# The opening of a 256-token block: constant matmuls while waiting, an early table load, and another order of the first units and pieces

## The reference, cut to what matters here

```python
def rms_norm(x, g):
    return x * rsqrt(mean(x * x) + 1e-6) * g

h = rms_norm(x, a_norm)                    # x: (1, 256, 1024)
u, z = split(h @ a_w_in, 2)                # a_w_in: 1024 x 2048
# pooled = windowed means of u, minus u
x = x + (mixed(pooled) * silu(z)) @ a_w_out
...                                        # gates, attention, S5, two MLPs follow
```

## Time and profile before

| | us |
|---|---|
| median of 3 runs | 898.32 |
| lowest and highest run | 893.40 and 901.04 |
| span of the profiled execution | 892.2 |

### The profile page before, as it was taken

One profiled execution on the slowest core, in us unless ns is written; L12 is line 12 of the kernel. 1 busy time (PEld: TensorE's weight loads), 2 busy tenths in 40 slices (PEclk: granted clock), 3 DMA queues, 4 the chain that ended last, 5 costly groups with the idle time before them and its releaser, 6 DMA issues.

```text
span 892.2 us, 13365 instructions
## 1 busy us (share of the span) xinstructions
PE 855.0 (96%) x5611; PEld 739.6 (83%) x5611; DVE 589.4 (66%) x739; ACT 441.0 (49%) x585; POOL 106.8 (12%) x73
## 2 busy tenths in 40 slices
PE   6999999899999999999899999997889999999998
PEld 4886888788788877878888888996778889999996
DVE  4684575676756668877768788774875655555553
ACT  5644466655953646644544445452064544444441
POOL 1000000211000013123033334330000000000000
PEclk9999999999999999999999999999899999999999
DMA  8936645365104436226455566557866555555521
GB/s 294 358 103 230 240 142 189 110 230 183 45 10 161 155 95 243 87 96 212 142 187 163 206 225 210 181 203 163 263 211 208 170 189 190 188 189 189 189 95 48
DMA packets 67253, 155.96 MB, mean 175 GB/s; under 512 B 3017, under 2 KB 6826, under 8 KB 66938
## 3 DMA queue, kind: packets, MB, share of 16 engines
q1 hardware_dynamic: 63888, 146.28, 48.7%
q0 software_dynamic: 2224, 7.67, 2.6%
q10 hardware_dynamic: 1082, 1.16, 0.6%
HBM read 146.70 MB, written 7.34 MB: 173 GB/s over the span
## 4 chain that ended last, share of the span: by engine, by line
PE 84%; DVE 10%; ACT 3%; DMA 2%; issue 1%; POOL 1%; ACTq 0%; DVEq 0%
PE bank L677 17%; PE bank L678 17%; PE bank L679 17%; PE bank L987 7%; PE bank L989 7%; PE bank L991 7%; PE bank L670 2%; PE bank L772 2%; DVE wlo L1572 2%; DVE wlo L1567 1%; DVE hT L1555 1%; ACT whi L1209 1%; PE bank L1052 1%; PE bank L762 1%; POOL rsh L2214 1%
## 5 line engine op out<-in xcount | busy, mean ns | idle before, releaser
L1572 DVE TENSOR_TENSOR wlo<-ring,whi 128x2048 fp32r<-128x2048 f32 (+1 forms) x105 | 256.9, 2450 | 141.7 <-ACT whi L1209 141.4
L1209 ACT ACTIVATE whi<-ring 128x2048 fp32r<-128x2048 f32 (+1 forms) x105 | 200.5, 1909 | 215.6 <-PE bank L679 147.8
L677 PE MATMUL bank<-whi,hT 128*128 128x512 f32 (+1 forms) x512 | 202.2, 395 | 5.1 <-DVE hT L2180 2.3
L679 PE MATMUL bank<-whi,hT 128*128 128x512 f32 (+1 forms) x512 | 199.8, 390 | 0.0
L678 PE MATMUL bank<-wlo,hT 128*128 128x512 f32 (+1 forms) x512 | 199.7, 390 | 0.0
L987 PE MATMUL bank<-hT,whi 128*128 128x256 f32 x512 | 145.8, 285 | 3.7 <-DVE aux L2101 2.9
L989 PE MATMUL bank<-hT,whi 128*128 128x256 f32 x512 | 144.8, 283 | 0.0
L991 PE MATMUL bank<-hT,wlo 128*128 128x256 f32 x512 | 144.8, 283 | 0.0
L677 PEld LDWEIGHTS bank<-whi,hT 128*128 128x128 f32 x512 | 96.8, 189 | 26.1 <-issue 4.4
L679 PEld LDWEIGHTS bank<-whi,hT 128*128 128x128 f32 x512 | 96.7, 189 | 19.8
L678 PEld LDWEIGHTS bank<-wlo,hT 128*128 128x128 f32 x512 | 96.9, 189 | 19.2 <-issue 0.2
(11 more groups left out here) (282 smaller groups left out, 1002.8 us busy)
## 6 DMA issues: line engine op xcount, KB each, us to landing
ring<-in_w_ff SPq DMA_DIRECT2D x64, 1024.0 KB, 5.4
ring<-in_ple_gate_w SPq DMA_DIRECT2D x8, 1024.0 KB, 5.1
ring<-in_w_kv SPq DMA_DIRECT2D x8, 1024.0 KB, 5.1
ring<-in_b_w_in SPq DMA_DIRECT2D x8, 1024.0 KB, 5.0
ring<-in_a_w_in SPq DMA_DIRECT2D x7, 1024.0 KB, 13.2
ring<-in_w_in SPq DMA_DIRECT2D x6, 1024.0 KB, 5.2
ring<-in_w_glu SPq DMA_DIRECT2D x6, 1024.0 KB, 6.6
ring<-in_a_w_out SPq DMA_DIRECT2D x4, 1024.0 KB, 5.9
```

The costliest lines, as they stand in the source:

```text
L677: pe.matmul(bank_cols, high[:, at[0], at[1]], w_high, start=first, stop=False)
L679: return pe.matmul(bank_cols, low[:, at[0], at[1]], w_high, start=False, stop=last)
L1209: act.activation(whi[at], raw_rows(g), ACT.Copy).then_inc(high_made, 1)
L1572: dve.tensor_tensor(wlo[at], raw_rows(g), whi[at], ALU.subtract).then_inc(low_made, 1)
```

## The change

- TensorE waits for `allneg` and runs 11 matmuls of 128 columns on it into bank 7, which nobody reads, ahead of its wait for the identity.
- The ACT queue issues the identity first, then the vectors. x's second half is now issued by SP, after the four pieces.
- ScalarE loads the table set right after its two DMA issues, and waits only for the copied gain vectors. It takes unit 0, piece 0, unit 1, piece 1, pieces 2 and 3, units 2 and 3. VectorE takes the same order.
- x units 2 and 3 are turned inside u block 0, after the first half of token tile 0.
- The three gains are scaled after the low parts of units 2 and 3, and ScalarE waits for them there, ahead of the second half of u block 0.

```diff
+WARM = 11
...
             for kk in range(4):
                 sp.dma_start(ring[:, 0, 512 * kk:512 * kk + 512], first[:, kk]).then_inc(piece_landed[kk], 16)
+            sp.dma_start(x[:, :, 512:D], w["x"].rearrange("b (t p) n -> p (b t) n", p=P)[:, :, 512:D])                .then_inc(x_half_landed[1], 16)
             sp.wait_ge(x_half_landed[1], 16)
...
+            pe.wait_ge(masks_ready, 1)
+            for n in range(WARM):
+                pe.matmul(ps[7][:, 0:P], allneg[:, :], allneg[:, :], start=True, stop=True, skip_group_check=True)
             pe.wait_ge(ident_landed, 16)
             pe.wait_ge(vecs_landed, 16)
...
-            turn("a", x, ready=lambda k: pe.wait_ge(x_half_landed[k // 2], 16))
+            def x_landed(k):
+                pe.wait_ge(x_half_landed[k // 2], 16)
+
+            turn("a", x, units=(0, 1), ready=x_landed)
             for stage in ("u", "za"):
                 for nb in range(2):
-                    product(stage, nb, (stage, nb), turned_by="a" if stage == "u" else None, pieces=(stage, nb) == ("u", 0))
+                    product(stage, nb, (stage, nb), turned_by="a" if stage == "u" else None, pieces=(stage, nb) == ("u", 0),
+                            first=(lambda: turn("a", x, units=(2, 3), ready=x_landed)) if (stage, nb) == ("u", 0) else None)
...
+            act.dma_start(cst[:, 0:P], w["tables"][:, 0:P]).then_inc(ident_landed, 16)
             act.dma_start(vrows[:, :], w["vecs"]).then_inc(vecs_landed, 16)
-            act.dma_start(cst[:, 0:P], w["tables"][:, 0:P]).then_inc(ident_landed, 16)
-            act.dma_start(x[:, :, 512:D], w["x"].rearrange("b (t p) n -> p (b t) n", p=P)[:, :, 512:D])\
-                .then_inc(x_half_landed[1], 16)
-            act.wait_ge(gains_ready, 3)
-            turned_high("a", "a_norm", (0, 1))
+            act.preload_act_table_set("natural_log_exp_and_others")
+            act.wait_ge(dve_emptied, u.emptied("vec"))
             for kk in range(4):
+                if kk < 2:
+                    turned_high("a", "a_norm", (kk,))
                 act.wait_ge(piece_landed[kk], 16)
                 ins = act.activation(whi[:, 0, 512 * kk:512 * kk + 512], ring[:, 0, 512 * kk:512 * kk + 512], ACT.Copy)
                 ins.then_inc(high_made if kk == 3 else piece_high, 1)
-                if kk == 1:
-                    turned_high("a", "a_norm", (2,))
-            turned_high("a", "a_norm", (3,))
+            turned_high("a", "a_norm", (2, 3))
+            act.wait_ge(gains_ready, 3)
             fill(1)
...
-            for name, scale in (("q_norm", HD ** -0.5), ("qn_moba", HD ** -0.5), ("qn_mla", MQK ** -0.5)):
-                dve.tensor_scalar(gain(name), gain(name), scale, None, ALU.mult).then_inc(gains_ready, 1)
-            dve.wait_ge(gains_ready, 3)
-            turned_low("a", "a_norm", (0, 1))
             for kk in range(4):
+                if kk < 2:
+                    turned_low("a", "a_norm", (kk,))
...
-                if kk == 1:
-                    turned_low("a", "a_norm", (2,))
-            turned_low("a", "a_norm", (3,))
+            turned_low("a", "a_norm", (2, 3))
+            for name, scale in (("q_norm", HD ** -0.5), ("qn_moba", HD ** -0.5), ("qn_mla", MQK ** -0.5)):
+                dve.tensor_scalar(gain(name), gain(name), scale, None, ALU.mult).then_inc(gains_ready, 1)
+            dve.wait_ge(gains_ready, 3)
             fill(1)
```

## The result

| | before | changed |
|---|---|---|
| median of 20 runs, us | 895.54 | 899.87 |
| lowest and highest run | 892.92, 906.36 | 895.95, 902.80 |
| span of the profiled execution | 892.2 | 901.0 |

The ratio is 1.0036, with a 95% interval of 1.0021 to 1.0050: 3.2 us slower (1.9 to 4.5), which is no change by the 1% bound. The forecast was 2.3 us slower. The plain medians lie 4.3 us apart; the ratio is the better measure, and the text goes by it. The two profiled executions differ by 8.8 us. As one run of each, they don't give the size of the change, so the first thing to settle is where in the span the 8.8 us lie.

What follows compares the result with a forecast made beforehand. TensorE, busy 96% of the span, was taken as the bound, so only its pauses matter. Span 892.2 + 0.4 + 1.85 = 894.45; the same 2.25 on the median 898.3 gave 900.6, range 892.5 to 904.5.

Steps and rivals of the forecast that it cites:

- B: Forecast case: matmul 25 waits for its split, the clock falls in that wait; 900.6 us, own range 900.4 to 901.6; chance 0.37.
- Constant matmuls, 0 on the path: Opening: eleven cost 2.4 to 4.7 us, hidden before the vectors land; up to 0.7 if the identity came by 5 us.
- Small loads, 6.65 us: Opening: identity first, vectors second; transposes start at 6.65 us, as the same queue place landed at 6.61 before.
- rival D: Vectors and identity land sooner, everything up to the split moves with them; faster, 897.0 us; chance 0.12.
- Table load, -1.28 us: Opening, ScalarE: the early activation table load leaves the chain, -1.28 us, and costs 0 in its new place.
- alternating order: Opening, units and pieces split in turn: first product matmul at 9.95 us, 2.6 us earlier than 12.54.
- x's second half at 9.8: Load issued by SP behind four pieces, at 3.13 instead of 1.82 us: taken to land at 9.8 us.
- k = 1 to 3 at the high level, unit 2 turned from 13.4: u block 0: k=1 starts at 11.35, 0.68 us for each k, k=3 ends at 13.4, then units 2 and 3 are turned.
- The wait ahead of matmul 25: u block 0: TensorE waits 4.2 us, 17.0 to 21.2, for the second half's split; 20.83 before, so +0.4 us.
- The fall in that wait: The clock falls in the 4.2 us idle time; work resumes on the low level for 3.7 us: +1.85 us.
- The rest at 0: Behind u block 0's second half: later split halves keep up and later refills only stand shorter in a full queue, cost 0.
- rule that was set against rows: The skill's rule that transposes don't count as TensorE being busy; the prediction counted them, and gave the rule 0.05 within C.

Runs made afterwards that it cites:

- both pauses filled: The changed kernel plus 16 constant matmuls behind u block 0's first half and 8 behind the turning of x units 0 and 1: ratio to before 1.0026.
- split first with a filled pause: Changed kernel: gains later, no wait before second half's load, that half split before units 2 and 3, 10 constant matmuls in front, 8 behind units 0 and 1: ratio 1.0017.

## Why the prediction was right

The median was 0.7 us below the forecast of 900.6, with the sign and the mechanism of its likeliest case (B), though below B's own range of 900.4 to 901.6. That it came so close in absolute time is luck. The forecast was added to 898.3, the median of 3 runs of before, and 20 runs gave 895.54; the change itself was forecast at 2.25 us and measured at 3.2 (1.9 to 4.5). Step by step:

- *Constant matmuls, 0 on the path.* Their length was right (22 records, done by 5.9 us), but they were not free: without them TensorE started at 5.06 us, so up to 0.85 us of the stream was in the open. The upper bound named for that, 0.7, was nearly exact. The clock was up only behind the fourth transpose, near 7.15; the sum had taken all of them at the high level, which was about 0.5 us too good.
- *Small loads, 6.65 us.* Wrong. They had landed by 5.06 to 5.66 us in three traces. The row of the second load in the queue (6.61) was the wrong neighbour: in before, half of x was issued right behind it on the same queue, and here nothing was. This is rival D's mechanism; the order of the two loads was swapped as well, and no run separates the two edits. It gave 0.75 us at the start and not the sign: 0.5 of it went in the transposes at the low level, the rest in the fall at 10.6.
- *Table load, -1.28 us; alternating order; x's second half at 9.8.* Load at 1.90, first product at 9.70 for 9.95, and SP's wait for x's second half was over at 9.86. Right.
- *k = 1 to 3 at the high level, unit 2 turned from 13.4.* The step that failed. The clock fell at 10.6, although TensorE's longest idle stretch was 2.07 us, so that six matmuls started 0.43 us apart and the turning began at 14.58. I had looked for falls only in pauses of over 3 us. The run with both pauses filled shows the size: 1.3 us at matmul 25, about the difference between 22.32 and the forecast 21.2.
- *The wait ahead of matmul 25.* Forecast 17.0 to 21.2; measured 18.35 to 22.32, 4.0 us, put down to VectorE's L1580. Its parts were right: gains 1.18 us, then 1.91 and 2.29.
- *The fall in that wait.* Forecast for 3.7 us behind matmul 25, 1.85 us lost. It lasted 5.3 us, 12 matmuls, 2.4 us: the term was sized 0.55 us too low.
- *The rest at 0.* No pause of TensorE from 22.32 to 60 us.

The opening lost 4.1 us where 2.25 had been forecast, and the timing gives 3.2. The errors had one sign but for the early start.

On the rule that was set against rows: the 16 transposes that raised the clock in the earlier trace rows were followed in the changed kernel by the same 16, at 633.03, at whose end it was still at 0.50 (above). In four of the 14 traces the clock rose while these transposes were TensorE's only work, and in five it stayed at 0.50 through them and the 256 small matmuls behind. So they can raise it and need not. The Trainium skill (TensorE: Matmul & The Clock Gate, Part 4: PE-mode transpose) says that they don't count as busy time in the same way. The four traces speak against it as a general rule, the five are no proof for it, and no run here was made to settle it.

## What to carry to other kernels

A head start in an opening is worth only what the next data allow: look first at which split or load the second stretch of work waits for, and how much it has to spare (here 1.9 us), before the first stretch is moved forward. Turning two units later saved TensorE a wait of its own, but put them in front of a longer chain on two other engines. And a pause that TensorE is given costs twice, once as itself and once as the matmuls behind it at half rate; filling two pauses with matmuls that nobody reads gave back 3.8 us of 4.1 in the opening (the timings don't resolve it), but in another kernel the filled pause only brought on a wait further back.

## What the runs showed of the hardware

- The clock fell behind idle stretches of only 2.07 us (changed, at 10.6) and 1.87 us (split first with a filled pause, at 19.3), each time about 1 us after work had begun again, and in a pause of 1.49 us (before + constant matmuls, at 8.9), where one of 2.3 us in the earlier trace rows had left it up. The length of a pause alone doesn't tell.
- From the first product matmul to the high level it took 5.7, about 5 and 2.3 us where nothing in the product's order differed (both traces of before, and before with the table load).
- Dense small matmuls need not bring the level up: 256 of 32 columns ran for 13.87 us at 0.50 from end to end in five traces. In the other nine the level rose at the end of the transposes ahead of them or within 1.7 us behind.
- Where two small loads were followed on their queue by half a megabyte, the second was there at 6.2 to 6.6 us; where nothing followed, and the smaller came second, both were there at 5.1 to 5.7.
